# Moving the context keys' product into the end of a down projection, and widening the modulation columns

## The chip, the cores and the metric

The kernel runs on one core of one Trainium2 chip. The metric is the device time of one execution in microseconds. Before the change the median of three runs is 1402.28 us (1400.53 to 1405.31).

## The reference

Two transformer blocks run one after the other over 512 tokens of width 1024. The first ends in a gated feed-forward layer. The second attends over its own tokens and over 256 context tokens, and its modulation vectors come from a small product with `w_mod`:

```python
# end of the first block
h = _rmsnorm(x, ffn_pre_norm[l])
u = _causal_depthwise_conv(h @ w_up[l], conv_w[l], conv_b[l])
gate, val = jnp.split(u, 2, axis=-1)
y = (jax.nn.gelu(gate, approximate=True) * val) @ w_down[l]
x = x + _rmsnorm(y, ffn_post_norm[l])

# start of the second block
sh1, sc1, gt1, sh2, sc2, gt2 = adaln(c, w_mod[l], b_mod[l])
csh1, csc1, ... = adaln(c_ctx, w_mod[l], b_mod[l])
h  = modulate(rmsnorm(x, g_pre1[l]), sh1, sc1)
hc = modulate(rmsnorm(ctx, g_pre1[l]), csh1, csc1)
q, k, v, f, g_a, g_f = split_proj(h @ w_in[l])     # q and k get axial rope
kc, vc = hc @ w_in[l][:, 512:640], hc @ w_in[l][:, 640:768]
attn = banded_window_attention(q, k, v, kc, vc, sink[l])
```

The context's normalised input `hc` does not depend on the first block, so the products for `kc` and `vc` can stand anywhere once `hc` is ready.

## The kernel before, in words

**Layout.** Activations lie with features over the 128 partitions and tokens along the row: `X`, `Y_A`, `Hhi`, `Hlo` are 8 chunks of 128 features by 512 tokens. A float32 product is done as three products in a faster 32-bit format, of high and low parts: high by high (line 351), low by high (352), high by low (353). Each weight chunk of 128x1024 comes by DMA into one of five buffers (`raw`), ScalarE makes its high part (line 301), VectorE its low part (line 317), and a buffer is free again when the chunk's products are done (`w_done`). Tokens are handled in two halves where a norm has to be waited for: "a" is tokens 0 to 255, "b" is 256 to 511. `PS` is PSUM, with 8 banks of 512 columns.

**Order.** Every engine has its own instruction list, written out by hand; the engines meet at counting semaphores. There is no scheduler: what stands behind a waiting instruction on its engine waits with it.

**End of the first down projection** (`down`, in the tensor, scalar and vector programs). Bank `o` sums the output chunk `o`. The last two input chunks are done bank by bank in the order `DN_ORDER` = 6, 7, 0 to 5, first for half "a", then for half "b". Half "a" is read by ScalarE, which writes the square of each bank into a buffer and copies the bank to `Y_A`; VectorE adds the squares up in `G_s` (`post_sum`, seven of them). Then VectorE copies half "b" of bank 6 to `Y_A` (semaphore `p_yb`), because TensorE needs bank 6 for the next thing: `post_stat`, a product of `G_s` with a matrix of ones (line 809), which sums the squares over partitions. TensorE has by then done half "b" of banks 6 and 7; it goes on with banks 0 to 5 after the statistic.

**Behind it.** ScalarE turns the statistic into a reciprocal root, VectorE adds the normalised half "a" to `X` (`residual`), ScalarE squares `X`, and TensorE sums those squares over partitions (`squares_sum`, line 907, bank 6). Between these sums stand the columns of modulation groups 4 and 5, and behind them the context's key product into bank 4 (`chunk_product` with `hcx`, width 256) and the statistic of half "b" into bank 6. Then come the grouped products of half "a" (`group_half_a`: keys and three query chunks), with the sums of squares of half "b" among them, the context's value product into bank 5, half "b" of the group, the value product of the block's own tokens (bank 4), the first rope product (`rope(0, K2)`, line 973), the columns of groups 6 to 9, and the fourth query chunk into bank 6 (`w_q3`). Rope products and Fourier chunks (`fill`, bank 7) follow.

**Columns.** The product with `w_mod` is done on VectorE, spread over earlier stages, into `macc`. What is left is a sum over partitions: `acc_columns` (line 566) multiplies a 128x128 piece of `macc` (as weights) with one column of ones, and so puts 128 sums into one PSUM column. A group has 4 such products per vector; groups 0 to 3 have two vectors, 4 to 11 one: 64 products in all. In the trace a float32 product of this kind shows as two records. Groups 0 to 3 stand in the first attention, 10 and 11 late in the second up projection. VectorE adds the bias to groups 4 to 9 at once (`mod_adds(4, 10, 7)`), after its first rope step.

Of the kernel before, what the change touches and what calls it, by code (L numbers as in the profile page):

```python
# [45 lines left out]
CH = {n: i for i, n in enumerate(_FIRST)}  # L46
# [7 lines left out]
def build(nc, a, out):  # L54
    f32, f32r, bf16 = mybir.dt.float32, mybir.dt.float32r, mybir.dt.bfloat16
    ALU, ACT, AX = mybir.AluOpType, mybir.ActivationFunctionType, mybir.AxisListType
# [25 lines left out]
    ones = at("ones", "K", kk + 512, [128, 128])  # L82
# [11 lines left out]
    def vc(name, i=0, n=1):  # L94
# [15 lines left out]
    G_a, G_b, G_c, G_d, G_r, G_s = (at(n, "G", 2048 * i, [128, T])  # L110
                                    for i, n in enumerate(("G_a", "G_b", "G_c", "G_d", "G_r", "G_s")))
# [40 lines left out]
    Y_A = at("Y_A", "A", 0, [128, 8, T])  # L152
# [9 lines left out]
    HChi = at("HChi", "M", 16384, [128, 8, 256], f32r)  # L162
    HClo = at("HClo", "M", 24576, [128, 8, 256], f32r)
# [16 lines left out]
    KC = at("KC", "A", 12288, [128, 256])  # L180
# [26 lines left out]
    PS = nc.alloc_psum_tensor("PS", [128, 8, T], f32).ap()  # L207
# [8 lines left out]
    q = Events()  # L216
# [5 lines left out]

    HALF = {"a": slice(0, 256), "b": slice(256, 512)}
    FULL = slice(0, T)

    DN_ORDER = (6, 7, 0, 1, 2, 3, 4, 5)

    PY = {0: 0, 1: 10, 2: 25, 3: 35}
    SQ = {0: 0, 1: 10, 2: 26, 3: 36}
    PA = {0: 0, 1: 9, 2: 23, 3: 32}  # L230
    XN = {0: 0, 1: 16, 2: 32, 3: 48}

    def nth(h):
        return 8 if h == "b" else 0
# [95 lines left out]
    def mod_sum(g, v):  # L330
        return macc4[:, g - 4, :] if 4 <= g < 8 else macc[:, v if g < 4 else g % 2, :]
# [6 lines left out]
    def wtile(i, k):  # L338
        return whi[i % NS][:, 128 * k:128 * k + 128], wlo[i % NS][:, 128 * k:128 * k + 128]
# [10 lines left out]
    def products(e, o, lhs, rhs, first, last, own=False):  # L350
        e.matmul(o, lhs[0], rhs[0], start=first, stop=False, skip_group_check=own)  # L351
        e.matmul(o, lhs[0], rhs[1], start=False, stop=False, skip_group_check=own)  # L352
        return e.matmul(o, lhs[1], rhs[0], start=False, stop=last, skip_group_check=own)  # L353

    def chunk_product(e, i, x, bank, ks=range(8), done=True, off=0, nk=8, width=T):
        e.wait_ge(q["w_lo"], i + 1)
        for k in ks:
            last = products(e, PS[:, bank, 0:width], wtile(i, off + k), x(k), k == 0, k == nk - 1)
        if done and ks[-1] == nk - 1:
            last.then_inc(q["w_done"], 1)  # L360
        return last
# [39 lines left out]
    for t in range(len(HALVES)):  # L401
        u = [u for s in range(t + 1) for p in range(2) for u in ENDS[s, p]][-1]
        n = UNITS[u]
# [4 lines left out]
    for t in range(len(HALVES)):  # L408
        u = [u for s in range(t + 1) for p in range(2) for u in ENDS[s, p] if (s, p) != (t, 1)][-1]
        n = UNITS[u]  # L410
# [150 lines left out]
    def tensor_program(e):  # L561
        def acc_columns(g, bank, at):
            e.wait_ge(q["mod_acc"], MOD_OPS[4 * g + 4])
            for n in range(4):
                for v in range(mod_vectors(g)):
                    last = e.matmul(PS[:, bank, at + 2 * n + v:at + 2 * n + v + 1], mod_sum(g, v)[:, 128 * n:128 * n + 128],  # L566
                                    ones[:, 0:1], start=True, stop=True)
            last.then_inc(q["mcol"], 1)


# [15 lines left out]
        for j in range(4):  # L586
# [7 lines left out]
            for k in range(4, 8):  # L594
                if j == 0:
                    e.wait_ge(q["h_lo"], k + 1)
                last = products(e, PS[:, j, :], wtile(j, k), hx(k), False, k == 7)
# [13 lines left out]
        for j in range(4):  # L611
            last = bias_part(j, PS[:, 6, 128 * j:128 * j + 128], 512, 640)
# [5 lines left out]
        for i in range(4):  # L618
            last = e.transpose(PS[:, 7, 128 * i:128 * i + 128], r1[:, 128 * i:128 * i + 128], ident)
# [187 lines left out]
        def post_stat(count, bank, cols):  # L807
            e.wait_ge(q["p_acc"], count)
            e.matmul(PS[:, bank, cols], ones, G_s[:, cols], start=True, stop=True).then_inc(q["stat"], 1)

        for o, h in O_LAST:
            b = o % 5
# [33 lines left out]
        for j in range(4):  # L846
            for k in range(6, 8):
                if j == 0:
                    e.wait_ge(q["h_lo"], 16 + k + 1)
                last = products(e, PS[:, j, HALF["b"]], wtile(CH["w_up"] + j, k), hxh(k, "b"), False, k == 7)  # L850
# [7 lines left out]
        for n in range(4, 2 * NF):  # L858
# [9 lines left out]
            if n == 19:  # L868
                ctx_sum(6)
                ctx_sum(7)  # L870

        def down(layer, i0, bank_free):
            for f in range(NF - 2):
                e.wait_ge(q["dd_lo"], NF * layer + f + 1)
                e.wait_ge(q["w_lo"], i0 + f + 1)
                for o in (6, 7, 2, 3, 4, 5, 0, 1):
                    if f == 0:
                        e.wait_ge(*bank_free[o])
                    last = products(e, PS[:, o, :], wtile(i0 + f, o), (Dhi[f % 4], Dlo[f % 4]), f == 0, False)
                last.then_inc(q["w_done"], 1)  # L880
            post = 2 * layer + 1
            for h in "ab":
                for i, o in enumerate(DN_ORDER):
                    if h == "b":
                        e.wait_ge(q["p_y"], PY[post] + i + 1)
                    for f in (NF - 2, NF - 1):
                        if h == "a" and i == 0:
                            e.wait_ge(q["dd_lo"], NF * layer + f + 1)
                            e.wait_ge(q["w_lo"], i0 + f + 1)
                        last = products(e, PS[:, o, HALF[h]], wtile(i0 + f, o),  # L890
                                        (Dhi[f % 4][:, HALF[h]], Dlo[f % 4][:, HALF[h]]), False, f == NF - 1, h == "b")
                        if h == "b" and i == 7:
                            last.then_inc(q["w_done"], 1)
                    if h == "a" or i < 7:
                        last.then_inc(q["dn_o"], 1)
                    if h == "b" and i == 1:
                        e.wait_ge(q["p_yb"], layer + 1)
                        post_stat(PA[post] + 7, 6, HALF["a"])

        e.wait_ge(q["r_ln"], RS["s"])  # L900
# [3 lines left out]

        def squares_sum(layer, h, c, sq):
            e.wait_ge(q["sq_a"], 16 * layer + nth(h) + c + 1)
            e.matmul(PS[:, 6, HALF[h]], ones, sq[c][:, HALF[h]], start=c == 0, stop=c == 7).then_inc(q["sq_mm"], 1)

# [31 lines left out]
                                    False, k == 7)  # L942
                last.then_inc(q["w_done"], 1)

        def hcx(k):
            return HChi[:, k, :], HClo[:, k, :]

        cK, cV = CH["w_k2"], CH["w_v2"]
        e.wait_ge(q["p_y"], PY[1] + 15)
        e.wait_ge(q["r_ln"], RS["p1a"])  # L950
        for c in range(8):
            squares_sum(0, "a", c, sq_a)
            if c == 2 or c == 4:
                acc_columns(3 + c // 2, 7, 8 * (c // 2 - 1))
        e.wait_ge(q["hc_lo"], 8)
        chunk_product(e, cK, hcx, 4, done=False, width=256).then_inc(q["kvc_mm"], 1)


        cs = [cK, CH["w_q2"], CH["w_q2"] + 1, CH["w_q2"] + 2]
        e.wait_ge(q["r_ln"], RS["n0a"])  # L960
        post_stat(PA[1] + 14, 6, HALF["b"])
        group_half_a(0, cs, sq_a)
        chunk_product(e, cV, hcx, 5, done=False, width=256).then_inc(q["kvc_mm"], 1)
        group_half_b(0, cs)

        def rope(i, x):
# [17 lines left out]
        e.wait_ge(q["kvc_ev"], 1)  # L984
        chunk_product(e, cV, hx, 4)
        rope(0, K2)
        for g in range(6, 10):
            acc_columns(g, 7, 8 * (g - 4))
        e.wait_ge(q["r_ln"], RS["n0b"])
        chunk_product(e, CH["w_q3"], hx, 6)  # L990
        rope(1, Q2[:, 0, :])
# [208 lines left out]
    def scalar_program(e):  # L1200
# [5 lines left out]
        def act(o, i, func, sem, **kw):  # L1206
            return e.activation(o, i, func, **kw).then_inc(q[sem], 1)  # L1207
# [33 lines left out]
        def rstd(dst, bank, cols, stat, n, norm):  # L1241
            e.wait_ge(stat, n)
            act(dst, PS[:, bank, cols], ACT.Ln, "r_ln", bias=epsc, scale=1.0 / D)
            e.wait_ge(q["r_ln"], RS[norm])
            act(dst, dst, ACT.Exp, "r", scale=-0.5)
# [139 lines left out]
        def post_rstd(norm, bank, cols):  # L1385
            rstd(G_r[:, cols], bank, cols, q["stat"], STAT[norm], norm)
# [116 lines left out]
            act(sq[c][:, HALF[h]], X[:, c, HALF[h]], ACT.Square, "sq_a")  # L1503

        def norm_rstd(layer, h):
            rstd(G_r[:, HALF[h]], 6, HALF[h], q["sq_mm"], 16 * layer + nth(h) + 8, f"n{layer}{h}")

        def normed(layer, h, c, shift):
            e.wait_ge(q["n_v"], 16 * layer + nth(h) + c + 1)
# [8 lines left out]
        for c in range(8):  # L1518
            normed(0, "a", c, MOD[:, c, 0:1])
            if c == 3:  # L1520
                post_rstd("p1b", 6, HALF["b"])
        split_to(CH["w_q3"])
        for c in range(8):
            squared(0, "b", c, sq_a)
# [3 lines left out]


        e.wait_ge(q["kvc_mm"], 1)  # L1530
        act(KC, PS[:, 4, 0:256], ACT.Copy, "kvc_ev")
        e.wait_ge(q["kvc_mm"], 2)
        act(VCt, PS[:, 5, 0:256], ACT.Copy, "kvc_ev")
        e.wait_ge(q["w_done"], CH["w_k2"] + 1)
# [171 lines left out]
    def vector_program(e):  # L1706
        ls = [0]

        def split_to(n):
            lo_to(e, ls, n)  # L1710
# [4 lines left out]
        def ts(o, x, s1, s2, op0, op1, sem):  # L1715
            return e.tensor_scalar(o, x, s1, s2, op0, op1).then_inc(q[sem], 1)
# [290 lines left out]
        def down(layer, i0):  # L2007
            prep_lo(layer, 2)
            for f in range(NF - 2):
                if f + 3 < NF:  # L2010
                    prep_lo(layer, f + 3)
                if layer == 0:
                    mod_part(D_MOD[f])
                split_to(i0 + f + AHEAD)
            split_to(i0 + NF - 2 + AHEAD)
            for i in range(1, 8):
                post_sum(2 * layer + 1, i, i, i, HALF["a"])
            o = DN_ORDER[0]
            e.wait_ge(q["dn_o"], 15 * layer + 9)
            ts(Y_A[:, o, HALF["b"]], PS[:, o, HALF["b"]], 1.0, 1.0, ALU.mult, ALU.mult, "p_yb")  # L2020

        def down_sums_b(layer, i0, i1):
            for i in range(i0, i1):
# [419 lines left out]
```

## Time and profile before

| what | value |
|---|---|
| median of the runs | 1402.28 us |
| profiled execution, its own time | 1401.24 us |
| its span, first to last instruction | 1399.5 us |
| TensorE busy | 1372.2 us |
| VectorE busy | 839.5 us |
| ScalarE busy | 636.2 us |
| mean granted TensorE clock | 0.993 |

The span is from the first to the last instruction of one execution, and times in rows are microseconds from its start. PE is the product side of TensorE and PEld its weight loads, which overlap; DVE is VectorE, ACT is ScalarE. In a timeline, instructions of one form that follow each other are merged (x8 is eight records), and the bracket at the end gives the idle time before and who ended it. The granted clock is a share of full speed: 1.00 is 2.4 GHz, 0.50 is 1.2 GHz.

### The profile page before, as it was taken

What the parts mean: (1) busy time and instruction counts of PE and PEld (TensorE: products, weight loads), DVE (VectorE), ACT (ScalarE), POOL (GpSimd) and SP (SyncE); (2) the same over time, 40 slices, a digit from 0 to 9 for tenths busy, and PEclk for the clock granted to TensorE, in tenths of its full rate; (3) what the DMA queues carried; (4) which work ended last, traced back from release to release, by engine and by line L of the source; (5) the groups of instructions that cost most, each with busy time, mean ns of one, the idle gap of its engine ahead of it and who ended that gap; (6) DMA issues with size and microseconds to landing.
All of it is one profiled execution on the core that took longest, in us unless ns stands there. A gap on an engine that the chain in (4) does not pass through costs nothing.

```text
span 1399.5 us, 17278 instructions
## 1 busy us (share of the span) xinstructions
PE 1372.2 (98%) x6886; PEld 1116.6 (80%) x6886; DVE 839.5 (60%) x1272; ACT 636.2 (45%) x1032; POOL 26.9 (2%) x28
## 2 busy tenths in 40 slices
PE   8999999999999999999999999999999999999998
PEld 6777766788888888888987777887888888888887
DVE  6577887487766767665846444346466543444334
ACT  7435566554545444234534544444544333333234
POOL 3000000000003000000000000000000000000000
PEclk9999999999999999999999999999999999999999
DMA  6524220323222333663031111132214432222321
GB/s 242 203 83 135 76 76 31 121 106 124 102 89 92 98 98 124 237 211 121 31 129 61 47 61 61 60 121 90 91 44 136 142 115 90 94 102 91 105 91 61
DMA packets 46043, 146.71 MB, mean 105 GB/s; under 512 B 4971, under 2 KB 12139, under 8 KB 45580
## 3 DMA queue, kind: packets, MB, share of 16 engines
q1 hardware_dynamic: 45676, 145.08, 31.3%
q8 instruction: 55, 0.90, 0.3%
q10 hardware_dynamic: 288, 0.52, 0.1%
q14 instruction: 24, 0.20, 0.0%
HBM read 142.18 MB, written 3.41 MB: 104 GB/s over the span
## 4 chain that ended last, share of the span: by engine, by line
PE 88%; DVE 6%; ACT 3%; DMA 2%; issue 1%; SPq 0%; DVEq 0%; ACTq 0%
PE PS L351 26%; PE PS L352 25%; PE PS L353 25%; PE PS L1056 1%; PE PS L1047 1%; DVE wlo L317 1%; DVE mt L1713 1%; PE PS L566 1%; PE PS L1021 1%; ACT whi L301 1%; PE PS L1029 1%; PE PS L722 1%; PE PS L668 1%; PE PS L673 1%; PE PS L657 1%
## 5 line engine op out<-in xcount | busy, mean ns | idle before, releaser
L317 DVE TENSOR_TENSOR wlo<-raw,whi 128x1024 fp32r<-128x1024 f32 x205 | 251.8, 1233 | 340.7 <-ACT whi L301 340.5
L351 PE MATMUL PS<-Hhi,whi 128*128 128x512 f32 (+1 forms) x1136 | 435.9, 384 | 7.7 <-DVE Hlo L1719 5.8
L352 PE MATMUL PS<-Hlo,whi 128*128 128x512 f32 (+1 forms) x1136 | 425.3, 374 | 0.0
L353 PE MATMUL PS<-Hhi,wlo 128*128 128x512 f32 (+1 forms) x1136 | 425.0, 374 | 0.0
L301 ACT ACTIVATE whi<-raw 128x1024 fp32r<-128x1024 f32 x205 | 215.1, 1054 | 241.6 <-DMA raw<-in_w_down 114.3
L351 PEld LDWEIGHTS PS<-Hhi,whi 128*128 128x128 f32 x1136 | 216.3, 190 | 59.9 <-issue 15.1
L353 PEld LDWEIGHTS PS<-Hhi,wlo 128*128 128x128 f32 x1136 | 216.4, 190 | 38.1
L352 PEld LDWEIGHTS PS<-Hlo,whi 128*128 128x128 f32 x1136 | 216.6, 191 | 36.5 <-issue 1.2
L351 PE MATMUL PS<-Dhi,whi 128*128 128x512 f32 (+1 forms) x384 | 142.9, 372 | 0.0
L352 PE MATMUL PS<-Dlo,whi 128*128 128x512 f32 (+1 forms) x384 | 142.6, 371 | 0.0
L353 PE MATMUL PS<-Dhi,wlo 128*128 128x512 f32 (+1 forms) x384 | 142.6, 371 | 0.0
L351 PEld LDWEIGHTS PS<-Dhi,whi 128*128 128x128 f32 x384 | 72.3, 188 | 12.7
L1719 DVE SCALAR_TENSOR_TENSOR macc<-wm,small,macc 128x512 f32<-128x512 f32 x112 | 80.8, 747 | 2.6 <-DMA wm<-in_w_mod 1.3
L353 PEld LDWEIGHTS PS<-Dhi,wlo 128*128 128x128 f32 x384 | 72.3, 188 | 12.6
L352 PEld LDWEIGHTS PS<-Dlo,whi 128*128 128x128 f32 x384 | 72.3, 188 | 12.4
L1207 ACT ACTIVATE C<-C 128x512 f32<-128x512 f32 x44 | 27.8, 633 | 70.0 <-DVE C L1719 69.9
L1207 ACT ACTIVATE PB<-PS,small 128x512 f32<-128x512 f32 (+1 forms) x32 | 23.4, 738 | 30.3 <-DVE small L1713 30.3
L1207 ACT ACTIVATE Dhi<-ACTV 128x512 fp32r<-128x512 f32 x44 | 27.4, 626 | 21.6 <-PE PS L353 21.5
L1207 ACT ACTIVATE C<-G_b,vec 128x512 f32<-128x512 f32 x22 | 18.0, 817 | 41.8 <-DVE G_b L1713 41.8
L1207 ACT ACTIVATE C<-G_a,vec 128x512 f32<-128x512 f32 x22 | 17.9, 816 | 40.3 <-DVE G_a L1713 40.3
L1713 DVE TENSOR_TENSOR Dlo<-ACTV,Dhi 128x512 fp32r<-128x512 f32 x44 | 30.1, 689 | 9.4 <-ACT Dhi L1207 9.3
L1719 DVE SCALAR_TENSOR_TENSOR C<-PS,vec,C 128x511 f32<-128x511 f32 x44 | 32.9, 747 | 0.8
(410 smaller groups left out, 1833.2 us busy)
## 6 DMA issues: line engine op xcount, KB each, us to landing
raw<-in_w_up SPq DMA_DIRECT2D x88, 512.0 KB, 3.5
wm<-in_w_mod SPq DMA_DIRECT2D x48, 512.0 KB, 3.7
raw<-in_w_down SPq DMA_DIRECT2D x44, 512.0 KB, 3.5
raw<-in_w_g SPq DMA_DIRECT2D x16, 512.0 KB, 3.4
raw<-in_w_out SPq DMA_DIRECT2D x8, 512.0 KB, 3.5
raw<-in_w_o SPq DMA_DIRECT2D x8, 384.0 KB, 3.4
raw<-in_w_sk SPq DMA_DIRECT2D x4, 512.0 KB, 4.5
raw<-in_w_dq SPq DMA_DIRECT2D x4, 512.0 KB, 4.7
```

Of the source, the lines that this page charges most:

```text
L301: e.activation(whi[i % NS], raw[i % NS], ACT.Copy).then_inc(q["w_hi"], 1)
L317: e.tensor_tensor(wlo[i % NS], raw[i % NS], whi[i % NS].bitcast(f32), ALU.subtract).then_inc(q["w_lo"], 1)
L351: e.matmul(o, lhs[0], rhs[0], start=first, stop=False, skip_group_check=own)
L352: e.matmul(o, lhs[0], rhs[1], start=False, stop=False, skip_group_check=own)
L353: return e.matmul(o, lhs[1], rhs[0], start=False, stop=last, skip_group_check=own)
L566: last = e.matmul(PS[:, bank, at + 2 * n + v:at + 2 * n + v + 1], mod_sum(g, v)[:, 128 * n:128 * n + 128], ones[:, 0:1], start=True, stop= ...
L657: last = e.matmul(PS[:, b + h, 0:w], QK[f"sk{j % 2}"][p, 128 * kb:128 * kb + 128], QK[f"sq{j % 2}"][p, 128 * kb:T], start=True, stop=True)
L668: last = e.matmul(PS[:, b + h, 0:w], trir, lparts(j, kb)[i][:, h, :], start=i == 0, stop=kb == 3 and i == 1)
L673: last = e.matmul(PS[:, b + h, o:w], onesr, lparts(j, jb)[i][:, h, :], start=False, stop=jb == 3 and i == 1)
L1207: return e.activation(o, i, func, **kw).then_inc(q[sem], 1)
L1713: return e.tensor_tensor(o, x, y, op).then_inc(q[sem], 1)
L1719: return e.scalar_tensor_tensor(o, x, s1, y, op0, op1).then_inc(q[sem], 1)
```

## The change

The key product of the context moves into the end of the first down projection, ahead of the statistic of half "a", and writes the second half of bank 6. So that bank 6's half "b" is free for it, VectorE's copy of that half comes after the first of the seven sums instead of after the last (only in the first of the two down projections). The sums of squares of half "b" and their statistic go to bank 4, which the keys no longer take. Columns 4 and 5 are done ahead of the sums of squares, where TensorE now waits for the copy of bank 7 (`PY[1] + 9`) and no longer for all banks; columns 6 to 9 come from behind the first rope product to right behind the sums of squares. Every column's product, in all twelve groups, streams 128 columns of ones instead of one and writes 128 equal columns, of which the next product overwrites all but the first.

```diff
+    SQ_BANK = {(0, "a"): 6, (0, "b"): 4, (1, "a"): 6, (1, "b"): 6}
...
# acc_columns
-                    last = e.matmul(PS[:, bank, at + 2 * n + v:at + 2 * n + v + 1], mod_sum(g, v)[:, 128 * n:128 * n + 128],
-                                    ones[:, 0:1], start=True, stop=True)
+                    last = e.matmul(PS[:, bank, at + 2 * n + v:at + 2 * n + v + 128], mod_sum(g, v)[:, 128 * n:128 * n + 128],
+                                    ones, start=True, stop=True)
...
+        def context_product(i, bank, cols):
+            e.wait_ge(q["hc_lo"], 8)
+            e.wait_ge(q["w_lo"], i + 1)
+            for k in range(8):
+                last = products(e, PS[:, bank, cols], wtile(i, k), hcx(k), k == 0, k == 7)
+            last.then_inc(q["kvc_mm"], 1)
...
# down, tensor program
                     if h == "b" and i == 1:
                         e.wait_ge(q["p_yb"], layer + 1)
+                        if layer == 0:
+                            context_product(CH["w_k2"], 6, HALF["b"])
                         post_stat(PA[post] + 7, 6, HALF["a"])
...
# squares_sum (and norm_rstd on ScalarE likewise)
-            e.matmul(PS[:, 6, HALF[h]], ones, sq[c][:, HALF[h]], ...
+            e.matmul(PS[:, SQ_BANK[layer, h], HALF[h]], ones, sq[c][:, HALF[h]], ...
...
-        e.wait_ge(q["p_y"], PY[1] + 15)
+        e.wait_ge(q["p_y"], PY[1] + 9)
+        acc_columns(4, 7, 0)
+        acc_columns(5, 7, 8)
         e.wait_ge(q["r_ln"], RS["p1a"])
         for c in range(8):
             squares_sum(0, "a", c, sq_a)
-            if c == 2 or c == 4:
-                acc_columns(3 + c // 2, 7, 8 * (c // 2 - 1))
-        e.wait_ge(q["hc_lo"], 8)
-        chunk_product(e, cK, hcx, 4, done=False, width=256).then_inc(q["kvc_mm"], 1)
+        for g in range(6, 10):
+            acc_columns(g, 7, 8 * (g - 4))
...
         e.wait_ge(q["r_ln"], RS["n0a"])
-        post_stat(PA[1] + 14, 6, HALF["b"])
+        e.wait_ge(q["p_y"], PY[1] + 15)
+        post_stat(PA[1] + 14, 4, HALF["b"])
         group_half_a(0, cs, sq_a)
-        chunk_product(e, cV, hcx, 5, done=False, width=256).then_inc(q["kvc_mm"], 1)
+        context_product(cV, 5, HALF["a"])
         group_half_b(0, cs)
...
         chunk_product(e, cV, hx, 4)
         rope(0, K2)
-        for g in range(6, 10):
-            acc_columns(g, 7, 8 * (g - 4))
         e.wait_ge(q["r_ln"], RS["n0b"])
         chunk_product(e, CH["w_q3"], hx, 6)
...
# scalar program
-                post_rstd("p1b", 6, HALF["b"])
+                post_rstd("p1b", 4, HALF["b"])
...
-        act(KC, PS[:, 4, 0:256], ACT.Copy, "kvc_ev")
+        act(KC, PS[:, 6, 256:512], ACT.Copy, "kvc_ev")
...
# down, vector program
+            def first_b():
+                o = DN_ORDER[0]
+                e.wait_ge(q["dn_o"], 15 * layer + 9)
+                ts(Y_A[:, o, HALF["b"]], PS[:, o, HALF["b"]], 1.0, 1.0, ALU.mult, ALU.mult, "p_yb")
+
             for i in range(1, 8):
                 post_sum(2 * layer + 1, i, i, i, HALF["a"])
-            o = DN_ORDER[0]
-            e.wait_ge(q["dn_o"], 15 * layer + 9)
-            ts(Y_A[:, o, HALF["b"]], PS[:, o, HALF["b"]], 1.0, 1.0, ALU.mult, ALU.mult, "p_yb")
+                if layer == 0 and i == 1:
+                    first_b()
+            if layer:
+                first_b()
```

## Rows read from the trace of the kernel before

**Rows 1.** The page, busy times: engine, busy us, share of the span, instructions.

```profile
PE 1372.2 (98%) x6886; PEld 1116.6 (80%) x6886; DVE 839.5 (60%) x1272; ACT 636.2 (45%) x1032; POOL 26.9 (2%) x28
```

**Rows 2.** Waits of TensorE, 711 to 900 us: in total, times, longest.

```profile
PE PS L351 <- ACT GT L1207: 0.7, 1, 0.7
```

**Rows 3.** Stretches: length, busy us per engine, granted clock, DMA share, GB/s.

```profile
658.00:661.20 3.20, 0.62 (x5) 0.40 (x3) 2.30 (x6) 2.59 (x9) 0.00 (x0) 1.00 0.00 0
...
665.80:672.00 6.20, 5.08 (x31) 4.75 (x32) 5.78 (x14) 4.49 (x11) 0.00 (x0) 1.00 0.52 169
...
711.80:715.80 4.00, 4.00 (x34) 4.00 (x32) 1.98 (x3) 2.96 (x3) 0.00 (x0) 0.85 0.52 193
715.80:721.60 5.80, 5.80 (x15) 4.53 (x15) 4.97 (x7) 1.17 (x2) 0.00 (x0) 0.52 0.00 0
```

**Rows 4.** Timeline of TensorE, 705 to 729 us: start, length, line, operation.

```profile
705.34 0.40 PE L351 MATMUL PS<-Hhi,whi 128*128 128x512 f32 x1
...
710.81 1.02 PE L973 MATMUL PS<-K,permc 128*128 128x512 f32 x2
711.67 4.15 PE L566 MATMUL PS<-ones,macc 128*128 128x1 f32 x32
715.68 0.77 PE L351 MATMUL PS<-Hhi,whi 128*128 128x512 f32 x1
...
723.93 1.02 PE L973 MATMUL PS<-Q,permc 128*128 128x512 f32 x2
...
728.22 1.02 PE L973 MATMUL PS<-Q,permc 128*128 128x512 f32 x2
```

**Rows 5.** Timeline of TensorE: one-column float32 products, then 128-wide ones.

```profile
1166.31 1.84 PE L566 MATMUL PS<-ones,macc 128*128 128x1 f32 x16
1168.01 0.49 PE L351 MATMUL PS<-Hhi,whi 128*128 128x512 f32 x1
...
117.40 1.05 PE L722 MATMUL PS<-DT,VD 128*128 128x128 f32 x8
118.20 0.30 PE L668 MATMUL PS<-L31hi,trir 128*128 128x128 f32 x1
```

**Rows 6.** Chain of waits, 657 to 661 us: start, length, work.

```profile
657.31 0.44 DVE G_s L1713
...
659.96 0.43 DVE G_s L1713
660.38 0.35 DVE Y_A L1716
...
660.77 0.71 PE PS L809 x2
```

**Rows 7.** Timeline of TensorE, 657 to 672 us.

```profile
657.19 0.28 PE L353 MATMUL PS<-Dhi,wlo 128*128 128x256 f32 x1
...
657.91 0.28 PE L353 MATMUL PS<-Dhi,wlo 128*128 128x256 f32 x1
...
665.49 0.28 PE L353 MATMUL PS<-Dhi,wlo 128*128 128x256 f32 x1
...
672.04 0.47 PE L351 MATMUL PS<-HChi,whi 128*128 128x256 f32 x1
```

**Rows 8.** Chain of waits, 675 to 690 us.

```profile
675.80 0.39 PE PS L351
...
689.28 1.73 PE PS L907 x8
```

**Rows 9.** Timeline of ScalarE, 670 to 717 us.

```profile
670.60 0.42 ACT L1207 ACTIVATE sq_m<-X 128x256 f32<-128x256 f32 x1 [0.44 <-DVE X L1719]
...
716.09 1.06 ACT L301 ACTIVATE whi<-raw 128x1024 fp32r<-128x1024 f32 x1 [0.18 <-DMA raw<-in_w_f]
```

**Rows 10.** Timeline of VectorE, 708 to 714 us.

```profile
708.73 1.22 DVE L317 TENSOR_TENSOR wlo<-raw,whi 128x1024 fp32r<-128x1024 f32 x1
...
713.19 0.69 DVE L1713 TENSOR_TENSOR K<-K,G_b 128x512 f32<-128x512 f32 x1
```

More of the change, by code:

```diff
@@ L870, in tensor_program, with hcx @@
                 ctx_sum(7)
+        def hcx(k):
+            return HChi[:, k, :], HClo[:, k, :]
+        def context_product(i, bank, cols):
[4 more added lines that the diff above has]
+            last.then_inc(q["kvc_mm"], 1)
         def down(layer, i0, bank_free):
@@ L906, in squares_sum @@
             e.wait_ge(q["sq_a"], 16 * layer + nth(h) + c + 1)
-            e.matmul(PS[:, 6, HALF[h]], ones, sq[c][:, HALF[h]], start=c == 0, stop=c == 7).then_inc(q["sq_mm"], 1)
+            e.matmul(PS[:, SQ_BANK[layer, h], HALF[h]], ones, sq[c][:, HALF[h]], start=c == 0, stop=c == 7).then_inc(q["sq_mm"], 1)
         def group_half_a(layer, cs, sq):
@@ L943, in group_half_b @@
                 last.then_inc(q["w_done"], 1)
-        def hcx(k):
-            return HChi[:, k, :], HClo[:, k, :]
         cK, cV = CH["w_k2"], CH["w_v2"]
-        e.wait_ge(q["p_y"], PY[1] + 15)
+        e.wait_ge(q["p_y"], PY[1] + 9)
+        acc_columns(4, 7, 0)
+        acc_columns(5, 7, 8)
         e.wait_ge(q["r_ln"], RS["p1a"])
@@ L1505, in norm_rstd @@
         def norm_rstd(layer, h):
-            rstd(G_r[:, HALF[h]], 6, HALF[h], q["sq_mm"], 16 * layer + nth(h) + 8, f"n{layer}{h}")
+            rstd(G_r[:, HALF[h]], SQ_BANK[layer, h], HALF[h], q["sq_mm"], 16 * layer + nth(h) + 8, f"n{layer}{h}")
         def normed(layer, h, c, shift):
```

## The prediction, made before the kernel was run

> **What bounds the kernel now.** I read the page's busy times first. TensorE is busy 98% of a 1399.5 us span [rows 1], so in most stages a change is worth what it takes off TensorE's own line of work. The waits of TensorE after the stage that changes come second: from 711 to 900 us it waits once, 0.7 us [rows 2], so whatever is saved before 730 us is carried forward by an engine that never waits for more than that. The table by stretch, with the granted clock, comes third [rows 3]. Two stretches matter. From 711.8 to 715.8 the columns of groups 6 to 9 run (16 products, 32 records of form 128x1) and the mean clock is 0.85; from 715.8 to 721.6 the query product behind them runs at 0.52, the 1.2 GHz level, although TensorE was busy all the time. At 658 to 661.2 it stood idle for 2.6 us of 3.2 and the clock stayed at 1.00. Last come timelines and the chain of waits around the end of the down projection, for the order in which things become ready.
>
> **1. Columns 6 to 9 leave the path after the first rope product.** They start at 711.67 and the query product behind them starts at 715.68 [rows 4]: 4.01 us go. At full clock they would have cost twice the 1.70 us of an 8-column pair (1166.31 to 1168.01 [rows 5]), 3.40 us; so 0.6 us of the 4.01 was the low clock.
>
> **2. The low clock behind them.** The value product before the stretch has the same 24 products, 512 wide, and takes 710.81 - 705.34 = 5.47 us. The query product takes 723.93 - 715.68 = 8.25 us [rows 4]. The difference, 2.78 us, is the half clock. The fall came during an unbroken run of one-column products. After the change the query product follows a 512-wide rope product and a full-rate value product directly, so I take it to run at 1.00. Bounds: 0 (the clock falls anyway) and 2.78; I take 2.78, since nowhere in rows 3 does the clock fall in a stretch of wide products.
>
> The Trainium skill (TensorE: Matmul & The Clock Gate, section "HAM oscillation") speaks against this: it puts the fall down to gaps in which TensorE is idle. Here the engine had no gap for microseconds before the fall, so the trace does not agree; by that rule the columns are not the cause, and term 2 may be nothing (rival B).
>
> **3. The price of a column.** A product 128x1 in float32 costs 1.70 / 8 = 0.213 us (two records each [rows 5]). A float32 product 128 wide is in the trace as well: four of them, 8 records, take 117.40 to 118.20, 0.20 us each [rows 5]. A 256-wide one costs 1.73 / 4 = 0.43 us [rows 8], half of which is 0.217. So a column costs 0.20 to 0.217 us either way. There are 64 columns: 24 (groups 4 to 9) are moved, 40 (groups 0 to 3, 10, 11) widen in place. Those 40 change by -0.5 to +0.2 us; I take 0.
>
> The same page (section "What overlaps and what doesn't") says that a weight load overlaps a running product only when the row groups differ. All these products use all rows, so by that rule a column would cost load plus stream (rival C). The 0.20 us row says that they overlap.
>
> **4. The end of the down projection.** Before, TensorE issues the last product of bank 7's second half at 657.91 [rows 7] and then stands until 660.77, when the sum of squares over the first half of the tokens starts [rows 6]. It waits for VectorE, which does seven sums and then the copy of bank 6 (0.35 us, 660.38). After, that copy is second: it can start when TensorE ends the six products of bank 6's second half, the last of which starts at 657.19 and is 0.28 long [rows 7], so 657.47 + 0.04 = 657.51. It frees VectorE at 657.86, and the second sum starts near 657.9 instead of 657.31. The chain of sums runs at 0.53 us ((659.96 - 657.31) / 5 [rows 6]); ScalarE's squares alternate two buffers with it and keep the same step, so nothing is caught up. The seventh sum starts at 660.55, ends at 660.98, and the statistic starts at 661.02: **+0.25 us**.
>
> The key product goes in between: 24 products 256 wide at 0.12 us ((657.91 - 657.19) / 6), 2.88 us, from about 658.0 to 660.9. Its weights and inputs were ready long before. It fits in the hole with 0.1 us to spare. Cover gone, it would cost what sticks out over 661.02.
>
> **5. From there to the first grouped product.** The +0.25 us goes through ScalarE's reciprocal root into VectorE's residual, sums, the weight split of the value chunk and the normalised rows, to TensorE's grouped product at 675.80 [rows 8]: 676.05 after. TensorE must be ready by then:
> - second half of the down projection: last product at 665.49 [rows 7], done issuing at 665.61 + 0.25 = 665.86;
> - columns 4 and 5, 8 x 0.213 = 1.70: 667.56;
> - eight sums of squares at 0.43. The first four are ready; the last waits for ScalarE's square (670.60 + 0.42 before [rows 9], 671.3 after) and ends at 671.75;
> - columns 6 to 9, 3.40: 675.15;
> - statistic into bank 4, 0.43: 675.6.
>
> That leaves 0.4 us. Before, the key product (from 672.04 [rows 7], some 2.9 us) filled this place; taking it away wins nothing by itself, since VectorE's chain sets 675.80, but it makes the room that the 3.40 us of columns need. The new banks (4 for the second half's sums and statistic, 6's second half for the keys) cost nothing: the readers come in the same order. The value product beside them only gains a wait on a split done long before. Term 5 is 0, between 0 and +0.9 (all 24 columns at 0.25, the rate of the slow stretch, less the slack).
>
> **6. What is late next.** The query product starts at 711.67 + 0.25 = 711.9 and ends at 717.4; its split was done at 709.95 [rows 10]. Then comes a rope product (711.67 - 710.81 = 0.86 [rows 4]) and the first Fourier chunk at 718.3. ScalarE's last of the four waiting splits ends at 717.15 + 0.25 [rows 9]. VectorE no longer waits for the columns: it does the small adds from 713.88 + 0.25 = 714.1 [rows 10], the four splits as ScalarE delivers them (about 1.2 each), and is free at 718.7, just as the rope product lands. The next rope product asks for VectorE's first rope step, near 719.4, and is due 728.22 - 723.93 = 4.29 us behind the one before it [rows 4], at 721.7. Slack 2.3 us; nothing is late.
>
> **Sum.** -4.01 - 2.78 + 0.25 = **-6.54 us** against the profiled execution's 1401.24 us (span 1399.5), so 1394.7. That execution lies 1.04 us under the median of the runs shown, 1402.28; the same distance gives **1395.7**.
>
> **The rivals.**
> A, the forecast: 1395.7, its own range 1394 to 1397.5. Chance 0.72.
> B, the clock falls all the same, either in the query product or further forward, in the loose stretch of squares and columns before 676. In the first case term 2 is lost: 1402.28 - 3.76 = 1398.5. In the second a fall as long as before (some 7 us at half rate, 3.4 us of work) lands where 0.4 us is free: -6.54 + 3.0, 1398.7. For it: the squares leave TensorE waiting for ScalarE. Against: the same stretch before had a 1.1 us gap, loose squares and one-column products, and held 1.00 [rows 3]. Chance 0.14.
> D, the lead is met by something that keeps its own time: the loads and splits of the Fourier chunks, or VectorE's rope steps behind them. It decides if VectorE is free later than 721.0 instead of 718.7, and would give back up to 3 us: about 1398. Against: the slack in step 6. Chance 0.09.
> C, the slower side: a wide column pays its load (0.106 per record) and then its stream (0.109 per record, half of a 256-wide one). The 40 columns in place then cost 80 x 0.109 = 8.7 us more, the 24 moved ones 48 x 0.109 = 5.2 less the 0.4 us of room and some 0.3 in the squares, 4.5: -6.54 + 13.2 = +6.7, **1409**. It decides from 0.05 us extra per record. Against: the 0.20 us row of step 3. Chance 0.05.
>
> **How the numbers follow.** The likeliest case gives 1395.7. The range takes A, the upper bounds of terms 3 and 5, and reaches to B and D: 1392.5 to 1399.3. A change under 0.3% (4.2 us, so above 1398.1) is about what a measurement here cannot tell from none. A gives 0.70 of its 0.72 to faster, B 0.04 and D 0.03; the rest of B and D is the same; C and a remainder are slower: faster 0.77, same 0.17, slower 0.06.
>
> **What would show it.** Steps 1, 2: the query product starts right after the rope product, takes 5.5 us, and no stretch between 700 and 725 is under 1.00. Step 3: the 8-column pair late in the second up projection still takes 1.7 us. Step 4: the keys' 24 products stand between 658 and 661, and the idle time before the statistic falls from 2.6 to about 0.1 us. Step 5: the grouped product starts at 676.0 to 676.1, released by VectorE and not by TensorE's own queue. Step 6: TensorE still waits under 1 us up to 900. The forecast is wrong if a new low-clock stretch appears, or if columns cost over 0.25 us.

## The result, and the profile after

| | before | after |
|---|---|---|
| median, 8 runs of each | 1400.77 us (1396.86 to 1405.31) | 1394.12 us (1391.79 to 1395.08) |
| profiled execution | 1401.24 us | 1394.65 us |
| its mean granted clock | 0.993 | 0.997 |

The ratio of after to before that came with the result is 0.9937, with a 95% interval of 0.9925 to 0.9949: faster by 7 to 10.5 us. The two medians alone differ by 6.7 us. Two repeats beside 24 and 23 runs of before (below) gave 0.9942 and 0.9934, so I go by 8 to 9 us. The forecast was 6.5. The direction and the mechanism held; the gain is about 2 us larger than forecast, for a term that the sum had put at 0 (step 3, below).

The page's busy times of after:

```profile
PE 1369.1 (98%) x6886; PEld 1113.9 (80%) x6886; DVE 839.2 (60%) x1272; ACT 635.5 (46%) x1032; POOL 26.9 (2%) x28
```

As many instructions as in [rows 1]. TensorE is busy 3.1 us less in a span that is 6.7 us shorter (1392.8), so about half of the difference between the two profiles is idle time that was filled. The stretches of [rows 3] in after, same columns, with two of the first attention ahead:

```profile
170.00:174.00 4.00, 3.74 (x26) 3.01 (x23) 1.55 (x4) 1.11 (x2) 0.00 (x0) 1.00 0.17 56
222.00:226.00 4.00, 3.98 (x30) 2.75 (x30) 2.32 (x6) 3.73 (x9) 0.00 (x0) 1.00 0.00 0
658.00:661.20 3.20, 3.20 (x28) 3.20 (x28) 2.46 (x6) 2.71 (x10) 0.00 (x0) 1.00 0.00 0
665.80:672.00 6.20, 6.01 (x38) 4.94 (x37) 5.85 (x16) 4.49 (x15) 0.00 (x0) 1.00 0.49 169
711.80:715.80 4.00, 4.00 (x17) 2.96 (x16) 2.92 (x7) 2.72 (x3) 0.00 (x0) 1.00 0.93 355
715.80:721.60 5.80, 5.80 (x25) 4.41 (x24) 5.77 (x7) 2.71 (x4) 0.00 (x0) 1.00 0.32 104
```

The hole at 658 (the stretch in which TensorE stood idle) is full, and neither stretch between 711 and 722 is below 1.00. Elsewhere falls of the clock stay in after, near 37 us (0.64 from 36 to 40) and near 1013 us (0.67 from 1012 to 1016). Of before, the same view has a fall at 222 that the prediction didn't look at:

```profile
222.00:226.00 4.00, 3.98 (x13) 1.66 (x12) 3.50 (x6) 1.86 (x8) 0.00 (x0) 0.63 0.00 0
```

The timeline of TensorE in after, for [rows 4, 7] and the end of the chain of [rows 8]:

```profile
658.67 0.28 PE L355 MATMUL PS<-Dhi,wlo 128*128 128x256 f32 x1
658.79 0.35 PE L353 MATMUL PS<-HChi,whi 128*128 128x256 f32 x1
...
661.73 0.48 PE L811 MATMUL PS<-G_s,ones 128*128 128x256 f32 x1
...
666.45 0.28 PE L355 MATMUL PS<-Dhi,wlo 128*128 128x256 f32 x1
666.57 1.95 PE L568 MATMUL PS<-ones,macc 128*128 128x128 f32 x16
...
672.02 0.70 PE L921 MATMUL PS<-sq_m,ones 128*128 128x256 f32 x2 [0.16 <-ACT sq_m L1217]
672.55 3.73 PE L568 MATMUL PS<-ones,macc 128*128 128x128 f32 x32
676.12 0.60 PE L811 MATMUL PS<-G_s,ones 128*128 128x256 f32 x2
676.74 0.39 PE L353 MATMUL PS<-Hhi,whi 128*128 128x256 f32 x1
...
711.76 1.02 PE L985 MATMUL PS<-K,permc 128*128 128x512 f32 x2
712.21 0.80 PE L353 MATMUL PS<-Hhi,whi 128*128 128x512 f32 x1
...
718.10 1.02 PE L985 MATMUL PS<-Q,permc 128*128 128x512 f32 x2
...
722.39 1.02 PE L985 MATMUL PS<-Q,permc 128*128 128x512 f32 x2
```

The keys' 24 products run from 658.79 to the statistic at 661.73. From the first rope product to the second it is 6.34 us; before it was 723.93 - 710.81 = 13.12 [rows 4]. The chain of waits of after, for [rows 8] (start, length, work):

```profile
672.72 3.57 PE PS L568 x32
676.29 0.43 PE PS L811 x2
676.72 0.02 issue
676.74 0.39 PE PS L353
```

The columns are now on the path up to the grouped product. The waits of TensorE from 705 to 893 us, for [rows 2], and VectorE's timeline, for [rows 6, 10]:

```profile
PE PS L353 <- ACT GT L1217: 0.7, 1, 0.7
```

```profile
658.27 0.42 DVE L1726 TENSOR_SCALAR Y_A<-PS 128x256 f32<-128x256 f32 x1 [0.39 <-PE PS L355]
...
661.25 0.43 DVE L1723 TENSOR_TENSOR G_s<-G_s,G_b 128x256 f32<-128x256 f32 x1
...
715.12 4.62 DVE L319 TENSOR_TENSOR wlo<-raw,whi 128x1024 fp32r<-128x1024 f32 x4
719.66 0.68 DVE L1723 TENSOR_TENSOR G_b<-PS,ropeS 128x512 f32<-128x512 f32 x1
```

VectorE is through the four splits at 719.7, 2.7 us ahead of the rope product at 722.39. Nothing gives the lead back.

### The profile page after: what moved, and what is told of

Its sections match the earlier page's. It is cut to its first block, busy times and chain, and to the rows that moved or that the text cites. A ratio compares the mean times of both kernels' runs of the same rounds, so it can differ in the third digit from the quotient of the medians.

```text
span 1392.8 us, 17279 instructions
## 1 busy us (share of the span) xinstructions
PE 1369.1 (98%) x6886; PEld 1113.9 (80%) x6886; DVE 839.2 (60%) x1272; ACT 635.5 (46%) x1032; POOL 26.9 (2%) x28
## 4 chain that ended last, share of the span: by engine, by line
PE 89%; DVE 6%; ACT 3%; issue 1%; DMA 1%; SPq 0%; DVEq 0%; ACTq 0%
PE PS L353 26%; PE PS L355 25%; PE PS L354 25%; PE PS L1066 1%; PE PS L1057 1%; DVE mt L1723 1%; DVE wlo L319 1%; PE PS L568 1%; PE PS L1031 1%; DVE X L1729 1%; PE PS L1039 1%; PE PS L724 1%; PE PS L675 1%; PE PS L670 1%; PE PS L659 1%
```

## The experiments

The table gives the time between landmarks of TensorE's timeline in every profile taken, in us: from the columns of group 2 to those of group 3 (both in the first attention; about 168 to 220 us), from there to the next sum of squares near 290 us, from the statistic near 660 us to the first rope product, and from there to the second. A star marks an interval in which the granted clock falls. "Second" and "third" are two more profiles of before. Behind each run below stand the median, the number of runs, and the ratio to runs of before on the same chip with its 95% interval.

| kernel | g2 to g3 | g3 to 290 | 660 to rope | rope to rope |
|---|---|---|---|---|
| before | 51.89 | 69.93* | 50.04 | 13.12* |
| before, second | 53.48* | 69.87* | 51.05* | 13.11* |
| before, third | 53.47* | 68.37 | 50.02 | 13.13* |
| keys_only | 51.88 | 70.02* | 51.54* | 11.49* |
| narrow_moved | 53.43* | 68.22 | 51.53* | 6.35 |
| streak_narrow | 51.90 | 69.83* | 50.04 | 13.13* |
| wide_late | 53.46* | 69.88* | 51.02* | 9.90 |
| after | 52.00 | 68.19 | 50.03 | 6.34 |
| after_again | 51.98 | 68.29 | 50.02 | 6.34 |
| after_third | 52.03 | 68.24 | 50.02 | 6.35 |
| wide_only | 52.01 | 68.21 | 50.98* | 9.90 |
| wide_again | 51.97 | 68.28 | 51.19* | 9.90 |
| wide_first | 51.98 | 68.27 | 51.17* | 13.12* |
| cols_only | 52.03 | 68.25 | 53.39* | 6.35 |
| streak_wide | 52.04 | 68.25 | 51.20* | 9.90 |
| filled | 52.01 | 68.26 | 50.03 | 6.35 |
| filled_again | 52.00 | 68.31 | 50.03 | 6.34 |
| wide_filled | 52.00 | 68.31 | 50.02 | 9.90 |

**The change again**, unchanged.

> The changed kernel once more, five rounds beside the kernel before. Theory 1 (the gain is the sum of the prediction: 4.0 us of columns off the path, 2.8 us of half clock behind them, 0.2 back at the statistic): 6.5 us faster, ratio 0.9953. Theory 2 (there is a further gain of some 2 us that the sum misses, as the ratio 0.9937 says): 8 to 9 us faster, and the profile shows a place outside 657 to 724 us that is shorter by about 2 us.

Median 1394.06 us (5 runs) against 1402.68 (24): 0.9942 [0.9927 to 0.9957].

**Widening alone**: before, with this one edit.

```diff
-  e.matmul(PS[:, bank, c:c + 1], mod_sum(...), ones[:, 0:1], ...)
+  e.matmul(PS[:, bank, c:c + 128], mod_sum(...), ones, ...)
```

> The kernel before, with nothing changed but the width of the columns: 128 instead of 1, all groups where they were. Theory 1 (the fall of the clock comes from the unbroken run of 16 one-column products): no fall after the first rope product, columns 6 to 9 take 3.4 us instead of 4.0 and the query product 5.5 instead of 8.3, 3.4 us faster (ratio 0.9976). Rival (the fall has another cause, idle time or chance): the clock falls again between 712 and 722 us, no difference. Rival C (a wide column pays load and stream): a pair of groups takes 3.4 instead of 1.7 us, 13 us slower.

1397.28 us (11 runs), 0.9973 [0.9963 to 0.9984]: 3.8 us by the ratio, 4.3 by the means (1402.11 and 1397.86), 3.4 expected. The timeline of TensorE shows the 16 products at the old place:

```profile
712.24 1.02 PE L973 MATMUL PS<-K,permc 128*128 128x512 f32 x2
713.10 3.73 PE L566 MATMUL PS<-ones,macc 128*128 128x128 f32 x32
...
722.14 1.02 PE L973 MATMUL PS<-Q,permc 128*128 128x512 f32 x2
```

3.73 us for 16 products, and the query product behind them at full speed: rival C (a load and a stream in turn) is ruled out, and 13.12 - 9.90 = 3.22 us come from the clock and the rate together, in this place alone. The rest, 0.6 to 1.0 us, lies elsewhere: by the table some 2.1 us are won between group 2 and the sum near 290, and some 0.6 given back behind the hole at 658 (50.98, where the three profiles of before have 50.37 in the mean).

**The change with narrow columns** (after, the edit above reversed).

> The changed kernel with one-column products again, in their new places. If the run of 16 one-column products is what lowers the clock, it falls now near 674 to 676 us, at the end of the columns, and the grouped product behind them runs some 6 us at half rate: 2.5 to 3.4 us of the gain are lost, 3 to 4 us faster than before. If the fall does not depend on the width, this is as fast as the changed kernel (6.5 faster), since the columns cost the same either way.

1397.43 us (6), 0.9971 [0.9957 to 0.9984]: 4.1 us by the ratio, 4.5 by the means, where 3 to 4 were expected. The stretch behind the moved narrow columns, and their timeline:

```profile
676.00:680.00 4.00, 4.00 (x21) 4.00 (x22) 3.86 (x9) 2.77 (x7) 0.00 (x0) 0.57 0.01 2
```

```profile
671.78 3.63 PE L568 MATMUL PS<-ones,macc 128*128 128x1 f32 x32
675.27 0.68 PE L811 MATMUL PS<-G_s,ones 128*128 128x256 f32 x2
...
676.51 0.41 PE L353 MATMUL PS<-Hhi,whi 128*128 128x256 f32 x1
```

The fall moves with the columns: the records of the grouped product are 0.41 us long where 0.28 is usual. That is rival B's second case, and it happens only with narrow columns. The total came near its expectation in part by luck: the fall costs 51.53 - 50.03 = 1.5 us, not 2.5 to 3.4. What else this kernel lacks against after is in the table too, a fall of 1.4 us behind group 2.

**The keys' move alone**: after, columns narrow, groups 4 and 5 back among the squares and 6 to 9 back behind the rope product.

```diff
+            if c == 2 or c == 4:
+                acc_columns(3 + c // 2, 7, 8 * (c // 2 - 1))
...
         rope(0, K2)
+        for g in range(6, 10):
+            acc_columns(g, 7, 8 * (g - 4))
```

> The keys' product inside the end of the down projection and its banks as in the change, but all columns one wide and at their old places. Theory: VectorE's chain sets the start of the grouped product, so taking 2.9 us off TensorE there wins nothing: 0.2 us slower (the late copy), same within noise; the clock still falls at 714. Rival (the keys' product was on the path): up to 2.9 us faster.

1401.95 us (12), 0.9998 [0.9987 to 1.0008]: nothing, as expected. In its profile the clock falls in two places instead of one: behind the squares near 678 (1.5 us more up to the rope product) and, shorter, behind the columns at 719 (1.6 us less up to the next). The expectation had only the second, at full length. The timeline of TensorE names who sets the grouped product:

```profile
677.55 0.39 PE L353 MATMUL PS<-Hhi,whi 128*128 128x256 f32 x1 [1.96 <-DVE Hlo L1729]
```

**The columns alone**: before with wide columns, 4 and 5 ahead of the squares, 6 to 9 behind them, the keys' product still behind those in bank 4.

> The kernel before with the columns' part of the change alone: 128 wide, groups 4 and 5 ahead of the squares, 6 to 9 behind them; the keys' product stays behind them in bank 4. TensorE's list ahead of the grouped product then holds 3.4 us of columns and 2.9 us of keys, 2.4 to 2.9 us more than VectorE's chain leaves. Theory: the whole gain of the columns less 2.4 to 2.7 us, so 2.5 us slower than the changed kernel and some 5.5 us faster than before; the wait of the grouped product on VectorE is gone. Rival (the room was not needed): as fast as the changed kernel.

1397.45 us (8) against 1401.54 (19): 0.9957 [0.9942 to 0.9973]. That is 6.0 us faster than before by the ratio and 4.9 by the means, where 5.5 were expected; against before, after gains 2.4 to 3.8 us more, by means. From 660 to the rope product it takes 53.39 us, 3.36 more than after. Not all of that is room: the hole at 658 stands empty here, a fall of the clock follows it, and TensorE's own work is on the chain of waits from there to the grouped product. In that chain 14 products take 0.21 us each instead of 0.12, and the statistic 0.91 instead of the 0.71 of [rows 6]: some 1.5 us. That leaves about 1.9 us for the room that step 5 named, where 2.4 to 2.7 were expected. So the keys' move is worth nothing alone, and over 3 us beneath the columns: some 1.9 us of room and 1.5 for the filled hole.

**A long run of columns.** Before, with the columns of groups 10 and 11 done four times over in the second up projection (24 more products, which nobody reads), once narrow and once with all columns wide.

```diff
+                for _ in range(3):
+                    streak(10, 6, 0)
+                    streak(11, 6, 8)
                 acc_columns(10, 6, 0)
```

> The kernel before with the columns of groups 10 and 11 done four times over, late in the second up projection where TensorE is always busy: 32 one-column products in a row instead of 8. 24 more products at 0.213 are 5.1 us of work. Theory (a long run of one-column products lowers the clock though TensorE is busy): the clock falls there and the time grows by more, 8 to 10 us. Rival (it was something else at 712 us): 5.1 us slower and the clock stays at 1.00.

> The same four times over, with all columns of the kernel 128 wide. Theory: no fall of the clock there; 5.1 us of work, less the 4 us that wide columns alone win elsewhere (measured 0.9973), so about 1 us slower than before. Against the narrow one this is 7 to 9 us faster; if the width had nothing to do with the clock, they would differ only by what width wins at 712 us.

Narrow: 1412.94 us (4), 1.0079 [1.0057 to 1.01], +11 us for 24 x 0.213 = 5.1 us of work (8 to 10 expected). Wide: 1403.93 us (10), 1.0015 [1.0005 to 1.0025], +2 us (1 expected), which is what the added work costs less what wide columns win elsewhere. In the place itself the profiles compare directly: from the first of these columns to the end it is 233.2 us in before, 244.9 with the narrow ones and 238.5 with the wide ones, so +11.7 and +5.3 us. Stretches of the narrow kernel, then its timeline:

```profile
1168.00:1172.00 4.00, 4.00 (x28) 4.00 (x28) 1.31 (x3) 1.69 (x2) 0.00 (x0) 0.72 0.35 128
1172.00:1176.00 4.00, 4.00 (x21) 4.00 (x20) 1.37 (x2) 0.00 (x0) 0.00 (x0) 0.50 0.00 0
```

```profile
1166.82 7.55 PE L574 MATMUL PS<-ones,macc 128*128 128x1 f32 x48
1174.23 3.55 PE L566 MATMUL PS<-ones,macc 128*128 128x1 f32 x16
1177.65 0.77 PE L351 MATMUL PS<-Hhi,whi 128*128 128x512 f32 x1
```

And the wide one:

```profile
1168.00:1172.00 4.00, 4.00 (x33) 3.79 (x32) 1.83 (x2) 0.32 (x1) 0.00 (x0) 1.00 0.00 0
```

```profile
1163.62 5.52 PE L574 MATMUL PS<-ones,macc 128*128 128x128 f32 x48
1168.98 1.95 PE L566 MATMUL PS<-ones,macc 128*128 128x128 f32 x16
1170.68 0.48 PE L351 MATMUL PS<-Hhi,whi 128*128 128x512 f32 x1
```

TensorE is busy 4.00 of 4.00 us in both. With one-column products the clock goes to 0.50 all the same; 32 products take 10.83 us. The wide ones take 7.06, 0.221 each, at 1.00. The two kernels differ here in nothing but the width, and this is what shows the cause. The Trainium skill (TensorE: Matmul & The Clock Gate, section "HAM oscillation") puts falls down to gaps of an idle engine; the trace does not agree here. Not every run of such products is followed by a fall: behind groups 0 and 1 and behind 10 and 11 (8 products each, as long as groups 2 and 3) there is none in any profile but the lengthened one.

**Where else the clock falls.** Two more profiles of before, and widening alone repeated with and without a filler in the hole at 658 (20 products 256 wide that nobody reads).

> The kernel before, one more profile, for where the clock falls. Theory 3 and the lower mean clock of its timed runs (0.992 against the profile's 0.993): beside the fall at 714 us there is one near 660 or 676 us in some profiles. Theory 1 alone: only the one of 3.4 us at 714.

> The kernel before, a second profile, as the first: a fall of the clock between 655 and 700 us beside the one at 714 under theory 3, none under theory 1 alone.

> The kernel with nothing changed but the width of the columns, once more, as the partner of the next one on the same chip: 3.4 to 4.3 us faster than before. Theory 3 (TensorE's hole at 658 us is itself followed by a fall of the clock in a part of the executions, which the prediction put at nothing): the profile shows a fall between 660 and 668 us more often than not. Rival: it does not.

> The same with twenty products 256 wide (2.4 us) that nobody reads in TensorE's hole ahead of the statistic at 658 to 661 us; the keys' product stays at its old place. Theory 3: no fall between 660 and 668 us, mean clock up by about 0.001, 1 to 1.7 us faster than the wide one alone, although useful work is the same. Rival (the fall there costs nothing since VectorE's chain is the bound, or does not come from the hole): the same time as the wide one alone within 0.5 us.

The second and third profile of before took 1405.25 and 1402.43 us, at a clock of 0.989 and 0.993. Stretches of the second:

```profile
170.00:174.00 4.00, 3.74 (x24) 3.20 (x21) 1.81 (x5) 0.96 (x2) 0.00 (x0) 0.81 0.09 27
...
226.00:230.00 4.00, 3.98 (x13) 1.99 (x13) 3.66 (x8) 2.10 (x7) 0.00 (x0) 0.64 0.00 0
...
664.00:668.00 4.00, 3.58 (x17) 3.40 (x17) 1.34 (x5) 2.44 (x8) 0.00 (x0) 0.57 0.00 0
```

Of these three falls the first profile of before had one. Wide_again: 1399.55 us (12), 0.998 [0.9969 to 0.9992], 2.8 us faster than before, less than the 3.4 to 4.3 expected. Wide_filled: 1397.65 (12), 0.9969 [0.9957 to 0.998], by means 1.8 us faster than wide_again. Their intervals overlap, so the times alone do not settle it; the profiles differ by 51.19 - 50.02 = 1.17 us here. The stretch behind the hole in wide_again, then in wide_filled:

```profile
664.00:668.00 4.00, 4.00 (x29) 4.00 (x29) 3.42 (x9) 3.19 (x12) 0.00 (x0) 0.78 0.00 0
```

```profile
660.00:664.00 4.00, 4.00 (x35) 3.98 (x35) 2.34 (x6) 3.73 (x13) 0.00 (x0) 1.00 0.00 0
```

A hole of 2.5 us is often followed by a fall that costs about 1 us (51.0 to 51.2 instead of 50.02 to 50.04): in seven of the ten profiles that keep the hole, and in none of the eight in which products fill it. In kind this is what the Trainium skill (TensorE: Matmul & The Clock Gate, section "HAM oscillation") says, a fall behind an idle gap, and here the trace agrees.

**The widening in halves**: before, with `w = 128 if g < 4 else 1` (wide_first), and its opposite (wide_late).

> The kernel before, with only the columns of groups 0 to 3 (first attention) 128 wide. Theory 4 (there too a run of 8 one-column products lowers the clock behind it, though less surely): no fall between 168 and 230 us, 1.5 to 2.5 us faster, the fall at 714 stays. Rival (those falls are chance and have nothing to do with the width): a fall at 172 or 224 us as in all profiles with one-column products, no difference in time.

> The kernel before, with only the columns of groups 4 to 11 wide. Theory 4: the query product behind columns 6 to 9 runs at full clock (3.2 us shorter), but a fall behind group 2 or 3 stays; less whatever the hole at 658 costs, 1.5 to 3 us faster. Together with wide_first it should make up what wide_only wins (3 to 4 us). Rival: all of it is here, 3 to 4 us faster.

Wide_first 1401.81 us (11), 0.9993 [0.9982 to 1.0003]; wide_late 1399.74 (11), 0.9982 [0.9971 to 0.9994]. The profiles separate them cleanly: wide_late keeps both falls in the first attention, wide_first has none. The times do so poorly. For wide_first 1.5 to 2.5 us were expected and the means give 0.8; its interval reaches to 2.5. Part of that is in the table: wide_first wins 2.1 us in the first attention, but the hole at 658 is followed by a fall, 51.17 us against 50.37 in the mean of before, and 0.8 us go back. Wide_late is 2.5 us faster by means, as expected.

**Filling two more holes**: after, with 9 and 11 products 512 wide that nobody reads, ahead of the waits near 293 and 1009 us.

```diff
+        filler(9, 5, MIX[1][0])
         e.wait_ge(q["r_ln"], RS["p0a"])
...
+        filler(11, 4, AThi[:, 1, :])
         e.wait_ge(q["p_y"], PY[3])
```

> The changed kernel with products that nobody reads in two holes of TensorE: nine 512 wide (2.0 us) at 293 us ahead of the statistic of the attention's output, eleven (2.5 us) at 1009 us ahead of the second block's grouped product. Both holes are followed by a fall of the clock in most profiles so far. Theory (idle or thin stretches lower the clock, whole products keep it up): both falls go, up to 1.7 us each, 1 to 3 us faster than the changed kernel. Rival: the falls stay or move, or the products end late and delay what waits: 0 to 1 us slower than the changed kernel.

> The changed kernel with the two holes filled, beside the changed kernel on one chip. Theory: the falls behind 293 and 1009 us go, 1 to 2 us faster than the changed kernel. Rival: equal within 0.5 us.

> The changed kernel on the same chip as these. By theories 1, 3 and 4 together: 6.8 less 0.2, plus about 2 for the falls behind groups 2 and 3 and 0.3 to 1 for the hole, 8 to 9.5 us faster than before; by the prediction's sum 6.5.

Filled: 1392.96 us (6), 0.993 [0.9915 to 0.9946]; again 1392.17 (5), 0.9925 [0.9912 to 0.9938]. After on the same chip as the second: 1393.2 (6), 0.9934 [0.9918 to 0.9951]. Filled is the fastest version run and its first profile has no fall at all. But neither has the profile of after_third, without any filler, and it is as fast (1390.67 us, filled_again 1390.79). The lead of 1.3 us over after by means is inside the intervals. The profiles tell the two holes apart. Filling the one at 293 wins nothing: from the sum near 290 to the statistic near 660 it is 371.2 us in after, which has no fall there, in after_again, which has one, and in both filled kernels. So a fall there costs nothing. Behind the hole at 1009 it does cost: from the second rope product to the columns of group 10 it is 441.5 to 442.5 us in the fourteen profiles with a fall and 440.1 to 440.6 in the four without, filled or not.

## Where the prediction was right, and the step that failed

The step that failed is step 3: the 40 columns that widen in place were put at 0 and gave some 2.1 us. The rest of the mechanism stands, with smaller misses in steps 4 and 5.

**Steps 1 and 2** (-4.01 and -2.78): met. The interval between the rope products shrank by 13.12 - 6.34 = 6.78 us; 6.79 was forecast. It is 6.34 or 6.35 in all three profiles of after and 13.1 in all three of before. Rival B's first case (the clock falls anyway in the query product) is refuted by these and by wide_only; its second is what narrow columns would have done.

**Step 3** (the 40 columns in place, 0): the mis-sized term. As a duration it was right to 0.01 us a product: the 8 columns of groups 10 and 11 take 1161.44 - 1159.74 = 1.70 us in after, as before. But groups 0 to 3 are one-column runs too, and what step 2 charged to the columns at 712 was not looked for there. In all seven profiles with those groups narrow the clock falls behind group 2, group 3 or both, at 1.5 to 1.7 us each; in none of the eleven with them wide. The mean of the first two intervals is 122.3 us over the three profiles of before and 120.2 over those of after: 2.1 us. The row at 222 was in the trace that I had; [rows 3] left it out.

**Step 4** (+0.25): the landmark distance from the sum near 290 to the statistic near 660 went from 371.01 to 371.22 us, +0.21. The keys' product stood out by next to nothing: it ends just ahead of the statistic at 661.73, and VectorE's last sum ends at 661.68. What failed is the reading that the hole leaves the clock at 1.00. It did in the profile that I read, and not in the second one, where a fall behind the hole costs 1.0 us. Over the three profiles of before this is 0.35 us.

**Step 5** (0): met in size, 676.74 - 661.73 = 15.01 us from the statistic to the grouped product, before 675.80 - 660.77 = 15.03. The releaser is another than the one named: TensorE's own columns, as the chain shows, not VectorE. All times here are 0.7 us later than forecast, like the statistic. Beyond that, by the chain, the columns start 0.26 us late (672.72 against 671.75 + 0.71) and take 3.57 us for 16, 0.223 each, not 3.40. That is 0.43 us, and it used up the slack of 0.4. The upper bound given for this term, +0.9, was added up wrongly: 24 columns at 0.25 are 0.9 more, and less the slack that is 0.5.

**Step 6**: right. One wait of 0.7 us up to 893; rival D would have needed VectorE free after 721.

The sum from profiles, means of three each: -6.78 - 2.1 - 0.35 + 0.2 = -9.0 us. The spans themselves differ by 9.9 (1401.2 and 1391.3). The other 0.8 lie between the second rope product and the columns of group 10, where nothing was changed; one of the three profiles of after happens to have no fall there, and the first one of before is slower there than the other two. The timed means differ by 7.3, 8.5 and 8.7 us in the three comparisons. The profile of before that I read had only one of the falls at 172, 227 and 664 us that the second has. That the profiled execution of after came out at 1394.65 us, where 1394.7 was forecast, is luck: before's happened to start its first columns 2.4 us earlier (67.64 against 70.04), ahead of everything that the change touches, and that hid what step 3 had missed. So is the agreement of the two medians of eight runs, 6.65 us apart: the ratios of all three comparisons put the gain at 8 to 9 us.

Open: why the hole at 658 is followed by a fall in one of the four profiles that keep it with all columns narrow, and in all six that keep it with columns widened; and why, of the four equally long runs in the first attention, only those of groups 2 and 3 are followed by one. The fall near 293 is in all seven profiles with groups 0 to 3 narrow and in two of the nine with them wide and the hole unfilled; it costs no time, and its tie to the columns is not explained.

## What to carry to other kernels

A run of one-column float32 products keeps TensorE busy by the profile and can still let its clock fall; 128 wide it takes the same time at full clock, and no wide run here was followed by a fall. So widen it wherever it stands, and look for the fall behind every such run before you price the edit. A move that is worth nothing by itself can be worth most of the moved work's length when it leaves a full stretch for a hole and others need the room. Where clock falls come and go between executions, one profile can undercount them: take three. And a fall can cost nothing, as the one near 293 us: measure the distance between landmarks around it before you spend work on it.

## What the runs showed that I had not expected

The same kernel loses clock in different places in each execution. The 89 runs of before beside the experiments spread from 1396.7 to 1405.8 us at mean clocks from 0.989 to 0.996, and the time follows the clock: the 15 at 0.989 average 1404.9 us, the 4 at 0.996 average 1398.0. A second source of spread is the start: the first columns begin between 67.4 and 70.5 us, in every kernel, ahead of all that was changed. A wide float32 product, two records with a load of 128 columns each, takes 0.20 us in a short run [rows 5] and 0.221 to 0.223 in runs of 16 and 32; one column alone takes 0.213 in a run of 8 [rows 5] and (675.27 - 671.78) / 16 = 0.218 in the run of 16 of narrow_moved. The width costs next to nothing. TensorE's holes are followed by a fall in some executions and not in others: the one of 2.3 us near 293 in 9 of the 16 profiles that keep it, the one of 2.5 to 2.6 us at 658 in 7 of 10, the one of 2.9 us near 1009 in 14 of 16.
